# The decays of a delta rule chunk made inside the chunk ahead of it, and its factor ahead of its scores' weights

## What is computed

```
gc = cumsum(g)                                   # within a chunk
dec_incl   = exp(gc[t] - gc[j]) for t >= j, else 0
dec_strict = the same for t > j
lmat = dec_strict * (k k^T) * beta[j]
u_v, w_k = solve(I + lmat, [v, exp(gc) * k])
attn  = dec_incl * (q k^T) * beta[j]
q_dec = exp(gc) * q
k_end = k * exp(gc[-1] - gc) * beta
# from chunk to chunk
u = u_v - w_k state
o = q_dec state + attn u
state = exp(gc[-1]) * state + k_end^T u
```

## Time and profile before

| | |
|---|---|
| median of 3 runs | 2125.66 us (2124.09 to 2133.22) |
| profiled execution | 2124.86 us, of which the span is 2123.1 us |
| TensorE matmul busy | 1994.7 us, 94% |
| TensorE weight load busy | 1595.6 us, 75% |
| VectorE busy | 1279.3 us, 60% |
| ScalarE busy | 809.4 us, 38% |
| mean granted TensorE clock | 0.972 of full |

### The profile page before, as it was taken

The page is one execution under the profiler, slowest core; times in us unless marked ns, Lnnn a source line. Parts: engine busy times, 40 slices in busy tenths (PEclk is TensorE's granted clock), DMA queues, the critical chain, the costliest instruction groups (busy, mean ns, idle before and its releaser), DMA issues.

```text
span 2123.1 us, 35657 instructions
## 1 busy us (share of the span) xinstructions
PE 1994.7 (94%) x15127; PEld 1595.6 (75%) x15127; DVE 1279.3 (60%) x2188; ACT 809.4 (38%) x1260; POOL 0.2 (0%) x4
## 2 busy tenths in 40 slices
PE   6998888889999998999999999999998799999997
PEld 5876555667788786788888888888887585887876
DVE  6622777556447575677777777767777634343433
ACT  4364333543224334434333344334344324332323
POOL 0000000000000000000000000000000000000000
PEclk9999889999999999999999999999999899999998
DMA  5330222325444332221211112211211041223321
GB/s 174 90 90 30 82 76 67 119 90 170 138 130 120 99 88 84 60 61 51 60 51 51 51 54 58 61 51 51 60 51 51 25 123 42 70 86 87 86 79 41
DMA packets 286640, 164.68 MB, mean 78 GB/s; under 512 B 6316, under 2 KB 283538, under 8 KB 286482
## 3 DMA queue, kind: packets, MB, share of 16 engines
q1 hardware_dynamic: 285972, 162.22, 26.0%
q10 hardware_dynamic: 510, 0.18, 0.0%
HBM read 160.29 MB, written 2.10 MB: 76 GB/s over the span
## 4 chain that ended last, share of the span: by engine, by line
PE 80%; DVE 12%; ACT 5%; issue 3%; DMA 0%; ACTq 0%; DVEq 0%
PE bank L464 20%; PE bank L466 18%; PE bank L465 18%; PE bank L481 2%; PE bank L483 2%; PE bank L482 2%; PE bank L864 2%; PE bank L1001 1%; PE bank L912 1%; ACT wh L1066 1%; PE bank L895 1%; DVE wl L1565 1%; PE bank L872 1%; PE bank L447 1%; PE bank L645 1%
## 5 line engine op out<-in xcount | busy, mean ns | idle before, releaser
L1565 DVE TENSOR_TENSOR wl<-stage,wh 128x1024 fp32r<-128x1024 f32 (+1 forms) x248 | 300.9, 1215 | 510.9 <-ACT wh L1066 510.9
L464 PE MATMUL bank<-hh,wh 128*128 128x512 f32 x1400 | 575.1, 411 | 11.0 <-DVE hl L1586 5.9
L1066 ACT ACTIVATE wh<-stage 128x1024 fp32r<-128x1024 f32 (+1 forms) x248 | 259.7, 1049 | 787.3 <-PE bank L466 483.7
L465 PE MATMUL bank<-hl,wh 128*128 128x512 f32 x1400 | 550.8, 393 | 0.0
L466 PE MATMUL bank<-hh,wl 128*128 128x512 f32 x1400 | 550.7, 393 | 0.0
L464 PEld LDWEIGHTS bank<-hh,wh 128*128 128x128 f32 x1400 | 265.0, 189 | 76.7 <-issue 15.9
L466 PEld LDWEIGHTS bank<-hh,wl 128*128 128x128 f32 x1400 | 265.3, 190 | 58.2
L465 PEld LDWEIGHTS bank<-hl,wh 128*128 128x128 f32 x1400 | 266.1, 190 | 48.3 <-issue 0.7
L464 PE MATMUL bank<-gh,wh 128*128 128x512 f32 x416 | 166.3, 400 | 17.1 <-DVE gl L1868 7.7
L466 PE MATMUL bank<-gh,wl 128*128 128x512 f32 x416 | 164.7, 396 | 0.0
L465 PE MATMUL bank<-gl,wh 128*128 128x512 f32 x416 | 164.6, 396 | 0.0
(11 more groups left out here) (363 smaller groups left out, 2662.8 us busy)
## 6 DMA issues: line engine op xcount, KB each, us to landing
stage<-in_hg_w_in SPq DMA_DIRECT2D x80, 512.0 KB, 3.7
stage<-in_ada_w SPq DMA_DIRECT2D x48, 512.0 KB, 4.2
stage<-in_w_up SPq DMA_DIRECT2D x44, 512.0 KB, 5.0
stage<-in_ft_w_in SPq DMA_DIRECT2D x32, 512.0 KB, 3.9
stage<-in_w_in SPq DMA_DIRECT2D x28, 512.0 KB, 3.8
stage<-in_w_down SPq DMA_DIRECT2D x16, 512.0 KB, 4.0
stage<-in_hg_w_out SPq DMA_DIRECT2D x16, 512.0 KB, 4.0
stage<-in_ft_w_out SPq DMA_DIRECT2D x16, 512.0 KB, 4.0
```

What stands on the lines that cost most here:

```text
L464: pe.matmul(bank[t % NLIN][:], wh[:, s, k, :], xh[:, k, :], start=a, stop=False)
L465: pe.matmul(bank[t % NLIN][:], wh[:, s, k, :], xl[:, k, :], start=False, stop=False)
L1066: do(A.activation(wh[:, l % NSPLIT, 0:nk, :], stage[:, u["slot"], 0:nk, :], ACT.Copy), "hi_ready")
L1565: do(X.tensor_tensor(wl[:, l % NSPLIT, 0:nk, :], stage[:, u["slot"], 0:nk, :], wh[:, l % NSPLIT, 0:nk, :].bitcast(F32), ALU.subtract), f"s ...
```

## The change

The rows, sums, differences, exponentials and factor of chunk c + 1 are made in the levels of chunk c, for c = 0 to 2: the rows behind level 2's copies on VectorE, the sums behind level 3's scores on TensorE (now into bank 6, which is free between `gkv` and the u products), the differences behind level 4's copies, the exponentials behind level 4's `weights` on ScalarE and ahead of its modulation copy, and the factor behind level 6's copy. Chunk 0 makes its own at its start as before, but it does so through the same functions. `ug` moves to a buffer of its own (`m0`), and the exponentials `eg` alternate between two buffers. TensorE waits for `eex` before the u products overwrite bank 6. And in every chunk `at_` is made behind `x1` and no longer ahead of it; VectorE now waits for `lt` itself before `x1`.

```diff
@@ -232,7 +232,12 @@

         names = ["ee", "eg", "at_", "lt", "m0", "m1", "xx", "xt", "tt", "vtok", "gk", "kend", "u", "wkT", "qdec", "st"]
         G = {n: at("g_" + n, 56 + 2 * i, [P, 4, P]) for i, n in enumerate(names)}
-        G["ug"] = G["tt"]
+
+        G["ug"] = G["m0"]
+
+        def decays(c):
+            return G["eg" if c % 2 == 0 else "m1"]
+
         oT = at("oT", 104, [P, 4, T])


@@ -661,14 +666,18 @@
                     turn(n - 1)


+            def decay_sums(c, b):
+                pe.wait_ge(S("ug"), c + 1)
+                for h in range(4):
+                    mm = pe.matmul(b[:, h * P:(h + 1) * P], ones[:], G["ug"][:, h, :], start=True, stop=True)
+                mm.then_inc(S("gr"), 1)
+
             scores(0)
             for c in range(TT):
                 tok = slice(c * P, (c + 1) * P)
                 n = 8 * c
-                pe.wait_ge(S("ug"), c + 1)
-                for h in range(4):
-                    mm = pe.matmul(bank[3][:, h * P:(h + 1) * P], ones[:], G["ug"][:, h, :], start=True, stop=True)
-                mm.then_inc(S("gr"), 1)
+                if c == 0:
+                    decay_sums(0, bank[3])
                 if c:
                     pe.wait_ge(S("o_ev"), c)
                     pe.wait_ge(S("st_upd"), c)
@@ -729,7 +738,12 @@
                                            G["xt"][:, h, to:to + w], start=True, stop=True)
                     mm.then_inc(S("XX"), 1)
                     scores(n + 1)
+                    if l == 3 and c < TT - 1:
+                        decay_sums(c + 1, bank[6])
                 n = 8 * c + 7
+                if c < TT - 1:
+
+                    pe.wait_ge(S("eex"), c + 2)
                 pe.wait_ge(S("x_upd"), 6 * c + 6)
                 for h in range(4):
                     pe.matmul(bank[6][:, h * P:(h + 1) * P], G["xt"][:, h, :], G["vtok"][:, h, :], start=True, stop=True)
@@ -1282,15 +1296,19 @@
                 if n in MOD_STEP:
                     mod_rows(MOD_STEP[n])

+            def decay_exps(c, b):
+                act.wait_ge(S("dif"), c + 1)
+                do(A.activation(G["ee"][:], G["ee"][:], ACT.Exp))
+                do(A.activation(decays(c)[:], heads4(b), ACT.Exp))
+                do(A.activation(kec[:, 4 * c:4 * c + 4], kec[:, 4 * c:4 * c + 4], ACT.Exp), "eex")
+
             for c in range(TT):
                 tok = slice(c * P, (c + 1) * P)
                 if c:
                     act.wait_ge(S("uw"), c)
                 do(A.activation(G["xt"][:], view(ident[:], [[0, 4], [1, P]]), ACT.Copy), "xt_one")
-                act.wait_ge(S("dif"), c + 1)
-                do(A.activation(G["ee"][:], G["ee"][:], ACT.Exp))
-                do(A.activation(G["eg"][:], heads4(bank[3]), ACT.Exp))
-                do(A.activation(kec[:, 4 * c:4 * c + 4], kec[:, 4 * c:4 * c + 4], ACT.Exp), "eex")
+                if c == 0:
+                    decay_exps(0, bank[3])
                 attention_tail(8 * c)
                 weights(8 * c)
                 act.wait_ge(S("x1T"), c + 1)
@@ -1301,6 +1319,8 @@
                     do(A.activation(G["tt"][:], heads4(bank[3]), ACT.Copy), "Te")
                     attention_tail(8 * c + l)
                     weights(8 * c + l)
+                    if l == 4 and c < TT - 1:
+                        decay_exps(c + 1, bank[6])
                     modulated(8 * c + l)
                 act.wait_ge(S("uw"), c + 1)
                 do(A.activation(G["u"][:], heads4(bank[6]), ACT.Copy))
@@ -1732,36 +1752,45 @@

             dve.wait_ge(S("gate_act"), 5)
             up = cst[:, 0:P]
-            for c in range(TT):
-                tok = slice(c * P, (c + 1) * P)
-                if c:
-                    dve.wait_ge(S("o_ev"), c)
+
+            def decay_rows(c):
                 for h in range(4):
                     do(X.tensor_scalar(G["ug"][:, h, :], up, ggc[:, 4 * c + h:4 * c + h + 1], None, ALU.mult),
                        "ug" if h == 3 else None)
+
+            def decay_differences(c, b):
                 dve.wait_ge(S("gr"), c + 1)
                 for h in range(4):
-
-                    do(X.tensor_scalar(G["ee"][:, h, :], bank[3][:, h * P:(h + 1) * P], gcc[:, 4 * c + h:4 * c + h + 1], 0.0,
+                    do(X.tensor_scalar(G["ee"][:, h, :], b[:, h * P:(h + 1) * P], gcc[:, 4 * c + h:4 * c + h + 1], 0.0,
                                        ALU.subtract, ALU.min))
-                do(X.tensor_tensor(kec[:, 4 * c:4 * c + 4], view(bank[3][:, 0:1], [[P, 4]], P - 1), gcc[:, 4 * c:4 * c + 4],
+                do(X.tensor_tensor(kec[:, 4 * c:4 * c + 4], view(b[:, 0:1], [[P, 4]], P - 1), gcc[:, 4 * c:4 * c + 4],
                                    ALU.subtract), "dif")
-                attention_tail(8 * c)
-                front(8 * c)
+
+            def decay_factors(c):
                 dve.wait_ge(S("eex"), c + 1)
                 for h in range(4):
                     do(X.scalar_tensor_tensor(G["ee"][:, h, :], G["ee"][:, h, :], beta[:, 4 * c + h:4 * c + h + 1], up,
                                               ALU.mult, ALU.mult))
                 do(X.tensor_tensor(kec[:, 4 * c:4 * c + 4], kec[:, 4 * c:4 * c + 4], beta[:, 4 * c:4 * c + 4], ALU.mult))
                 do.settle()
+
+            for c in range(TT):
+                tok = slice(c * P, (c + 1) * P)
+                if c == 0:
+                    decay_rows(0)
+                    decay_differences(0, bank[3])
+                attention_tail(8 * c)
+                front(8 * c)
+                if c == 0:
+                    decay_factors(0)
                 dve.wait_ge(S("kk"), c + 1)
                 b4, b5 = (bank[i][:].rearrange("p (h c) -> p h c", c=P) for i in (4, 5))

                 do(X.scalar_tensor_tensor(G["lt"][:], G["ee"][:], -1.0, b4, ALU.mult, ALU.mult))
-                do(X.tensor_tensor(G["at_"][:], G["ee"][:], b5, ALU.mult))
-                do.settle(1)
+                do.settle()
                 dve.wait_ge(S("xt_one"), c + 1)
                 do(X.copy_predicated(G["xt"][:], view(gmask[:, 0, :], [[0, 4], [1, P]]), G["lt"][:]), "x1")
+                do(X.tensor_tensor(G["at_"][:], G["ee"][:], b5, ALU.mult))

                 dve.wait_ge(S("vk"), c + 1)
                 for h in range(4):
@@ -1769,7 +1798,7 @@
                     do(X.tensor_scalar(G["gk"][:, h, :], bank[3][:, h * P:(h + 1) * P], egc[:, i:i + 1], None, ALU.mult))
                     do(X.tensor_scalar(G["kend"][:, h, :], bank[3][:, h * P:(h + 1) * P], kec[:, i:i + 1], None, ALU.mult))
                 do(X.tensor_copy(G["vtok"][:], bank[6][:].rearrange("p (h c) -> p h c", c=P)), "gkv")
-                do(X.tensor_tensor(G["qdec"][:], qkv[:, 0:4, tok], G["eg"][:], ALU.mult))
+                do(X.tensor_tensor(G["qdec"][:], qkv[:, 0:4, tok], decays(c)[:], ALU.mult))

                 for l in range(1, 7):
                     attention_tail(8 * c + l)
@@ -1783,6 +1812,13 @@
                         do(X.copy_predicated(G["xt"][:], mask, b5), "x_upd")
                     else:
                         do(X.tensor_copy(G["xt"][0:64, :, 64:P], b5[0:64, :, 64:P]), "x_upd")
+                    if c < TT - 1:
+                        if l == 2:
+                            decay_rows(c + 1)
+                        if l == 4:
+                            decay_differences(c + 1, bank[6])
+                        if l == 6:
+                            decay_factors(c + 1)
                 attention_tail(8 * c + 7)
                 front(8 * c + 7)
                 dve.wait_ge(S("uwe"), c + 1)
@@ -1797,7 +1833,7 @@
                         do(X.tensor_copy(G["st"][:], b5), "st_upd")
                     else:
                         for h in range(4):
-                            do(X.scalar_tensor_tensor(G["st"][:, h, :], G["st"][:, h, :], G["eg"][:, h, P - 1:P],
+                            do(X.scalar_tensor_tensor(G["st"][:, h, :], G["st"][:, h, :], decays(c)[:, h, P - 1:P],
                                                       bank[5][:, h * P:(h + 1) * P], ALU.mult, ALU.add),
                                "st_upd" if h == 3 else None)
             attention_tail(32)
```

## The result

The changed kernel takes 2142.46 us in the median of 7 runs (2137.36 to 2147.37), the kernel before 2125.66 in 7 runs beside them. The ratio is 1.0069, with a 95% interval of 1.0053 to 1.0085: 0.7% slower, where 0.15% had been forecast. The profiled execution took 2139.31.

A forecast was written before the change was run, and what follows sets the result against it. TensorE is nearly always busy overall, but the affected stage was taken as a chain passing between engines with none full. -10.7 + 0.4 + 2.4 + 3.0 + 8.0 = +3.1 us gave 2128.8 us, range 2120.0 to 2136.0.

The forecast's parts named there:

- The starts: Starts of chunks 1 to 3: scores' weights come earlier by 3.3, 3.7 and 3.7 us, together 10.7 saved.
- that wait: Chunk start, `x1` now waiting for `lt` itself: about 0.1 us exposed, four times, 0.4 in all.
- The rows in level 2: Level 2, chunks 0 to 2: four VectorE operations that nothing covers, 0.8 us each chunk, 2.4 in all.
- The four sums: Level 3 on TensorE: 0 in chunk 0, 1.8 in chunk 1, 1.2 in chunk 2; 3.0 us, bounds 0 and 5.4.
- The factors in level 6: Level 6, five VectorE operations of 1.2 us, covered by VectorE's 1.93 us idle before `u`: cost 0.
- the level 4 part: Differences and exponentials delay level 5's Te and modulation columns, 2.65 us a chunk, 8.0 in all; TensorE idles about 2.6.
- the whole cost: Level 4: the 2.65 us lateness exceeds VectorE's own 1.1, so it counts alone and isn't added to it.
- rival C: Level 5's stall lowers TensorE's clock over levels 5 and 6, three chunks: 6.0 us more, +9.1, 2134.8; chance 0.13.
- B: TensorE's clock stays up at the chunk's start: value products save 6.6 us, -3.5 in all, 2122.2; chance 0.12.
- The remark that the stage's stretches show no engine full: Delta-rule and attention stage: no engine is full, work passes from engine to engine; so the timeline was used.
- A: Level 4's stall mostly hidden, only VectorE's slots paid, 3.3 for 8.0: -4.6 in all, 2121.1; chance 0.10.
- D: Chunk start: key products start no earlier, most of the 10.7 lost, +13.8 stays, 2139.5; chance 0.03.

The follow-up runs named there:

- e2: Changed kernel plus nine unread TensorE products in level 5 of chunks 0 to 2, no wait touched: 2128.66 us, ratio 1.0015.
- e1: Changed kernel with the next chunk's exponentials behind level 5's weights instead of level 4's: 2132.06 us, ratio to the kernel before 1.0016.
- e7: Kernel before plus nine unread products behind k's transposes and three behind the modulation at every chunk's start: 2120.4 us, ratio 0.9975.
- e8: Changed kernel with decay work moved out of the levels, plus four and five unread products at every chunk's start: 2110.59 us, ratio 0.9926.
- e9: Kernel before with six ScalarE copies behind level 4's weights and nine unread TensorE products in level 5, chunks 0 to 2: 2137.29 us, ratio 1.0049.
- e3: Kernel before with only six ScalarE copies added behind level 4's weights in chunks 0 to 2: 2144.13 us, ratio 1.0086.
- e6: Changed kernel with exponentials behind level 5's weights, plus four unread products in levels 3 and 5 of chunks 0 to 2: 2124.95 us, ratio 0.9985.

## Why the prediction was wrong

**The sum's waits and slots held.** The starts gave 10.68 for 10.7. `lt` starts at the end of the key products and `x1` starts 302.77 - 302.05 = 0.72 after `lt`, 0.11 more than L1761 did, as estimated, so that wait isn't free. The rows in level 2 made TensorE wait 1.07 for 0.17 in front of level 3's turn in chunk 0 and 1.52 for 0.72 in chunk 1, which is their 0.8 uncovered. The four sums fitted into chunk 0's idle; in chunk 1 level 3's turn to level 4's took 6.53 for 4.86, 1.7 for the 1.8 forecast. TensorE stood 2.52 idle ahead of level 5's columns in all three chunks for the 2.6 forecast. The factors in level 6 were hidden, with `u` released by TensorE in chunk 1 and the closing stretch no longer in e2 than before. From the L447 of chunk 1 to that of chunk 2 (L452 now) it took 298.53 - 246.57 = 51.96, where 48.6 had been forecast.

**The step that failed is the last claim of the level 4 part, that the stall is "the whole cost"**, and with it rival C's price and chance. C named the mechanism, the clock coming down in level 5, but priced it at 1.0 a level, 6.0 in all for levels 5 and 6, with 0.13 for its chance, and the forecast's sum had nothing for it. Its condition for more, that the low clock reach the closing products, was met in all three chunks: there L749 took 2.07 for 1.16. Columns to `st` cost 4.96, 3.95 and 7.70, 16.6 in all: from the columns to L749, which is levels 5 and 6, 3.2, 2.6 and 2.9 (8.7 for C's 6.0), and from L749 to `st` 1.7, 1.4 and 4.8 (7.9 for nothing). What I held against C, many matmuls on either side of the idle, didn't protect it. The kernel before showed the pattern already: the clock at 0.50 behind the thin start, and the turn of level 4 in chunk 1 at 1.12 for 0.66, amid many matmuls. I took this as a chance for a gain (B) and not as a warning for the stall that I had just worked out. The Trainium skill, "TensorE: Matmul & The Clock Gate", section "HAM oscillation — how this bites in real kernels", tells of waits for DMA between bursts and of each burst starting slow. The waits that it describes are longer than the 2.52 us here; what follows this shorter one was at 0.50 in 232 to 240 all the same. The remark that the stage's stretches show no engine full doesn't hold either: TensorE was busy 4.00 of 4 us in 252 to 256, at the lower level.

**Of the rivals.** A did not come: the stall was there in full. e1 removed ScalarE's part of it by an edit, and `lt` to level 5's columns fell by 7.5 us in the profiled executions, but much of the slow clock behind them stayed. B came true in chunk 2 alone of the changed kernel, in e7 and e8 in every chunk. D can be dropped, as the starts show. Of the range, 2120 to 2136, the high end took C's small price and so lay 6.5 below the median.

**What stays open.** How long the low level lasts differs: it ended before the output in chunk 1 (columns to `st` +3.95) and lasted through it in chunk 2 (+7.70). No run here tells what decides that. That `at_` and `x1` change places wasn't tried by itself.

## What to carry to other kernels

When a change makes TensorE wait in the middle of its work, price the stretch behind the wait at the lower clock, and not the wait alone: here 7 to 9 us of waiting brought 8 to 12 us of slow clock (e9 and e3). Work that is moved ahead to shorten one wait belongs where its engine already waits for another, which the timeline's idle brackets name (VectorE 3.04 us ahead of the state's update, ScalarE 3.16 ahead of the output copy), and not into a ring of levels in which each engine is late in turn. If the idle can't be avoided, products that nobody reads are a cheap cover, where a bank is free for them (e2, e6, e7).

## What had not been expected of the hardware

Short idles were enough. In chunk 0 of e1 TensorE stood idle 1.07 us ahead of level 3's turn and 1.19 ahead of level 5's, was busy on both sides of each, and the clock was at 0.50 a few us later; with both filled (e6) it stayed at 1.00 through the chunk. The length of one idle doesn't decide it: in chunk 0 of e8 TensorE paused 1.18 us at about 230.5, and the clock stayed at 1.00 from 228 to 256.

In e7's profiled execution, which at 2126.85 was the slowest of its runs, TensorE paused 1.67 us inside a group of products in chunk 1, waiting for nothing that the profile shows, and then ran slow although every start was filled:

```profile
266.69 0.34 PE L730 MATMUL bank<-g_tt,g_xt 128*64 128x64 f32 x4
268.70 0.88 PE L730 MATMUL bank<-g_tt,g_xt 128*64 128x64 f32 x12 [1.67 <-issue]
...
271.94 1.11 PE L718 MATMUL bank<-g_xx,g_lt 128*64 128x64 f32 x8
```

From `lt` to `st` that chunk took 45.37, against 39.38 in the kernel before, where it had no such pause. What the pause is, the trace doesn't say. It may be one way in which one execution is several us slower than the next with the same instructions; that was not followed up.
